# Differential attention on one Trainium2 core: score rows read in two-bank pieces, the one-piece maximum left by the read, lambda multiplied on GpSimd

## The reference, cut to what matters

```python
def _diff_attention(q, k, v, lq1, lk1, lq2, lk2, g_sub, lambda_init):   # 4 heads, 2 components of width 64, L = 2064
    lam = exp(sum(lq1 * lk1)) - exp(sum(lq2 * lk2)) + lambda_init
    def blk(qp, q1b, q2b):                       # 128 query rows at a time
        bias = where(mask, -slopes * dist, NEG)  # chunk-causal mask, ALiBi
        s1 = einsum('bhqd,bhkd->bhqk', q1b, k1) * scale + bias
        s2 = einsum('bhqd,bhkd->bhqk', q2b, k2) * scale + bias
        a = softmax(s1) - lam * softmax(s2)
        return einsum('bhqk,bhkv->bhqv', a, v)
```

## Time and profile before

| what | us |
|---|---|
| median of three runs (lowest, highest) | 2634.56 (2634.42, 2636.75) |
| profiled execution, its own time | 2637.24 |
| its span | 2635.5 |
| PE busy, share of the span | 2570.9, 98% |
| DVE busy | 1620.1, 61% |
| ACT busy | 1211.2, 46% |
| POOL busy | 334.1, 13% |
| differential attention | 460 to 828 |

### The profile page before, as it was taken

How to read it: one execution, slowest core, us unless ns; L and a number is a source line. 1 busy time by engine, 2 the same in 40 slices (tenths; PEclk the granted TensorE clock), 3 DMA queues, 4 the chain that set the end, 5 groups by cost and what they waited for, 6 DMA issues and landing times.

```text
span 2635.5 us, 35377 instructions
## 1 busy us (share of the span) xinstructions
PE 2570.9 (98%) x12220; PEld 2115.3 (80%) x12220; DVE 1620.1 (61%) x3488; ACT 1211.2 (46%) x2177; POOL 334.1 (13%) x366
## 2 busy tenths in 40 slices
PE   8999999899998999999999999999999999999998
PEld 8998787666676888877877888888888888888886
DVE  6223304989995766763458777777767565564665
ACT  6112312677775555554445333443335353343554
POOL 2110001222221222220000000000000001111133
PEclk9999999899999999999999999999999999999999
DMA  7324456633533011016576677666746355676787
GB/s 228 126 105 123 114 167 231 152 92 86 125 133 92 29 45 41 25 60 189 176 247 203 209 237 226 216 180 206 225 118 218 108 210 120 154 179 153 202 169 136
DMA packets 331516, 398.85 MB, mean 151 GB/s; under 512 B 23488, under 2 KB 237744, under 8 KB 323024
## 3 DMA queue, kind: packets, MB, share of 16 engines
q1 hardware_dynamic: 313776, 364.68, 44.1%
q0 software_dynamic: 17568, 31.99, 8.4%
HBM read 240.13 MB, written 156.48 MB: 150 GB/s over the span
## 4 chain that ended last, share of the span: by engine, by line
PE 62%; DVE 2%; DMA 1%; ACT 1%; issue 1%; SPq 0%; POOL 0%; DVEq 0%; ACTq 0%; POOLq 0%
PE ff_ps_x L3165 25%; PE ff_ps_m L3165 13%; PE ff_ps_z L3165 6%; PE ml_ps_s L2042 6%; PE ff_ps_m L1602 4%; PE ml_ps_o L2071 4%; PE ml_ps_t L2055 2%; DMA ml_v_raw<-scr_yT 1%; DMA ff_pieces<-scr_acc 0%; PE ff_ps_r L2602 0%; PE mo_ps_t L2619 0%; SPq L2229 0%; DVE ff_pieces L2332 0%; DVE ff_pieces L2523 0%; DVE ff_pieces L2519 0%
## 5 line engine op out<-in xcount | busy, mean ns | idle before, releaser
L3165 PE MATMUL ff_ps_x<-ff_mv_hi_p,ff_st_hi_p 128*128 128x512 f32 x764 | 297.9, 390 | 0.5 <-ACT ff_u L2905 0.5
L3165 PE MATMUL ff_ps_x<-ff_mv_hi_p,ff_st_lo_p 128*128 128x512 f32 x764 | 297.3, 389 | 0.0
L3165 PE MATMUL ff_ps_x<-ff_mv_lo_p,ff_st_hi_p 128*128 128x512 f32 x764 | 297.2, 389 | 0.0
L2042 PE MATMUL ml_ps_s<-wide,ml_qs 128*128 128x416 f32 (+14 forms) x880 | 197.9, 359 | 2.9 <-PEq L137 2.7
L3011 DVE TENSOR_TENSOR ff_st_lo_p<-ff_ps_m,ff_st_hi_p 128x512 fp32r<-128x512 f32 x190 | 130.6, 688 | 103.7 <-ACT ff_st_hi_p L2888 103.7
L2855 POOL DMA_DIRECT2D scr_acc<-ff_pieces x64 | 55.5, 872 | 1015.3 <-DVE ff_pieces L3035 946.8
L2905 ACT ACTIVATE ff_u<-ff_ps_x 128x512 f32<-128x512 f32 x128 | 76.6, 598 | 214.7 <-PE ff_ps_x L3165 214.7
L3165 PEld LDWEIGHTS ff_ps_x<-ff_mv_hi_p,ff_st_hi_p 128*128 128x128 f32 x764 | 143.4, 188 | 32.4 <-issue 2.0
L2042 PEld LDWEIGHTS ml_ps_s<-wide,ml_qs 128*128 128x128 f32 x880 | 152.5, 193 | 18.8 <-issue 7.4
L3165 PEld LDWEIGHTS ff_ps_x<-ff_mv_hi_p,ff_st_lo_p 128*128 128x128 f32 x764 | 143.4, 188 | 29.9
L3165 PEld LDWEIGHTS ff_ps_x<-ff_mv_lo_p,ff_st_hi_p 128*128 128x128 f32 x764 | 143.4, 188 | 29.6
(11 more groups left out here) (300 smaller groups left out, 6370.1 us busy)
## 6 DMA issues: line engine op xcount, KB each, us to landing
st_raw<-in_w_ff SPq DMA_DIRECT2D x64, 512.0 KB, 6.3
scr_hid<-ff_pieces SPq DMA_DIRECT2D x128, 256.0 KB, 2.6
st_raw<-scr_hid SPq DMA_DIRECT2D x64, 512.0 KB, 5.2
ring<-in_w_ff SPq DMA_DIRECT2D x28, 1024.0 KB, 7.8
scr_t<-ring SPq DMA_DIRECT2D x24, 1024.0 KB, 6.4
ring<-scr_t SPq DMA_DIRECT2D x21, 1024.0 KB, 7.9
scr_acc<-ff_pieces POOLq DMA_DIRECT2D x64, 256.0 KB, 4.0
ring<-scr_u SPq DMA_DIRECT2D x13, 1024.0 KB, 8.5
```

The lines of the kernel that those rows point to most:

```text
L2042: m = pe.matmul(ps_s[n % NSB][:, 0:w], q, k, start=j == 0, stop=j == len(pairs) - 1)
L3165: m = pe.matmul(bank[:, :], w[kind][:, k], a[kind][:, k], start=start and k == 0 and i == 0, stop=stop and k == KH - 1 and i == 2, skip_gr ...
```

## The change

Rows are cut by `row_pieces` into pieces of at most 1024 columns, two banks: 1 for rows 0 to 6, 2 for 7 to 14, 3 for row 15; 26 per component, 52 per head. `NSB` is 2, each of 1024 columns, so the scores still take four banks. `bank_parts` splits a piece wider than 512 into two parts on either side of the bank border, for which PE runs two matmuls each, with one semaphore for the piece; DVE reads both banks in one instruction. The read scales by -scale and takes the minimum, so that for one-piece rows its accumulator is `nmax` itself, and ACT waits for the read; rows of several pieces keep the combining instruction. The second sum is inverted in a step of its own (`ratio`, `RATIO_AFTER` 2), and POOL multiplies it by -lambda. `SCALE_AFTER` is 1 and `END_AFTER` 3, counted in pieces, and pending steps of earlier rows are put in only at the end of component 1. A piece costs w + 120 in the planner, before w + 60.

```diff
+def row_pieces(i):
+    width = META + P * (i + 1)
+    n = -(-width // 1024)
+    step = -(-width // n // 32) * 32
+    return [(c, min(step, width - c)) for c in range(0, width, step)]
+
+def bank_parts(w):
+    if w <= 512:
+        return 0, [(0, w)]
+    front = -(-w // 64) * 32
+    return 512 - front, [(0, front), (front, w - front)]
...
-        NSB = 4
-        ps_s = [mem.ps(f"da_ps_s{i}") for i in range(NSB)]
+        NSB = 2
+        ps_s = [mem.ps(f"da_ps_s{i}", 1024) for i in range(NSB)]
...
+        in_pieces = [(i, c) for i in range(NT) for c in range(COMPS) if len(row_pieces(i)) > 1]
...
-                        steps += [step for _, step in later if step[2] - NT * step[1] < i]
-                        later = [(left, step) for left, step in later if step[2] - NT * step[1] >= i]
+                        if c == COMPS - 1:
+                            steps += [step for _, step in later if step[2] - NT * step[1] < i]
+                            later = [(left, step) for left, step in later if step[2] - NT * step[1] >= i]
                         later.append((1, ("exp", 0, i, c)))
                         if c == 0:
                             later.append((SCALE_AFTER, ("scale", 0, i)))
                         if c == COMPS - 1:
+                            later.append((RATIO_AFTER, ("ratio", 0, i)))
                             later.append((END_AFTER, ("end", 0, i)))
...
-                return chunks[step[2]][3] + 60
+                return chunks[step[2]][3] + 120
...
-        SCALE_AFTER, END_AFTER = 2, 5
+        SCALE_AFTER, RATIO_AFTER, END_AFTER = 1, 2, 3
...
+            def ratio(h, i, **at):
+                if isinstance(h, int) and (h, i) == (0, 0):
+                    pool.wait_ge(lam_step, 4)
+                hold(pool, inv2_made, NT * h + i + 1)
+                pool.tensor_scalar(inv2[:, i % 2:i % 2 + 1], inv[:, i % 2, 1:2], lam[:, 3:4], 1.0, ALU.mult, ALU.mult).then_inc(ratio_ready, 1)
...
-                act.wait_ge(max_ready, NT * COMPS * h + COMPS * i + c + 1)
-                act.activation(comp_row(i, c, u), comp_row(i, c, u), ACT.Exp, bias=nmax[:, i % 2, c:c + 1], scale=scale,
+                if (i, c) in in_pieces:
+                    act.wait_ge(max_ready, len(in_pieces) * h + in_pieces.index((i, c)) + 1)
+                else:
+                    act.wait_ge(scores_read, NCH * h + [chunk[:2] for chunk in chunks].index((i, c)) + 1)
+                act.activation(comp_row(i, c, u), comp_row(i, c, u), ACT.Exp, bias=nmax[:, i % 2, c:c + 1], scale=-1.0,
...
+                if c == 1 and k0 == 0 and not (first_head and i < 2):
+                    dve.wait_ge(probs_ready, NT * h + i - 1)
+                least = mx[:, i % 2, c, nth:nth + 1] if (i, c) in in_pieces else nmax[:, i % 2, c:c + 1]
+                s0 = bank_parts(w)[0]
...
-                if k0 + w == META + P * (i + 1):
+                dve.tensor_tensor_reduce(out=comp_row(i, c, u)[:, k0:k0 + w], in0=ps_s[n % NSB][:, s0:s0 + w],
+                                         in1=bias[u][:, b0:b0 + w], scale=-scale, scalar=-LOWEST,
+                                         op0=ALU.add, op1=ALU.min, accum_out=least).then_inc(scores_read, 1)
+                if k0 + w == META + P * (i + 1) and (i, c) in in_pieces:
...
-                dve.tensor_scalar(inv2[:, i % 2:i % 2 + 1], inv[:, i % 2, 1:2], lam[:, 3:4], None, ALU.mult).then_inc(inv2_step, 1)
-                dve.wait_ge(inv2_step, n + 2)
+                dve.reciprocal(inv[:, i % 2, 1:2], total[:, i % 2, 1:2]).then_inc(inv2_made, 1)
+
+            def end(h, i, u, **at):
                 dve.wait_ge(first_scaled, NT * h + i + 1)
+                dve.wait_ge(ratio_ready, NT * h + i + 1)
...
-                for j in range(2):
-                    m = pe.matmul(ps_s[n % NSB][:, 0:w], qs[:, g % 2, c, P * b:P * b + P], keys[u][:, 2 * c + j, k0:k0 + w],
-                                  start=j == 0, stop=j == 1)
+                s0, parts = bank_parts(w)
+                for a, size in parts:
+                    for j in range(2):
+                        m = pe.matmul(ps_s[n % NSB][:, s0 + a:s0 + a + size], qs[:, g % 2, c, P * b:P * b + P],
+                                      keys[u][:, 2 * c + j, k0 + a:k0 + a + size], start=j == 0, stop=j == 1)
```

More of the change, by code:

```diff
@@ L1160, in attention @@
         inv_ready, first_scaled, probs_ready = (mem.sem(f"da_{s}") for s in ("inv_ready", "first_scaled", "probs_ready"))
-        inv2_step = mem.sem("da_inv2_step")
+        inv2_made, ratio_ready = mem.sem("da_inv2_made"), mem.sem("da_ratio_ready")
         pT_ready, pv_done = mem.sem(f"da_pT_ready"), mem.sem("da_pv_done")
@@ L1165, in attention @@
         o_stored = ahead.o_stored
-        chunks = [(i, c, k0, n) for i in range(NT) for c in range(COMPS) for k0, n in row_chunks(i)]
+        chunks = [(i, c, k0, n) for i in range(NT) for c in range(COMPS) for k0, n in row_pieces(i)]
         NCH = len(chunks)
+        in_pieces = [(i, c) for i in range(NT) for c in range(COMPS) if len(row_pieces(i)) > 1]
         tiles_of = lambda g: 1 + 4 * (g + 1)
@@ L1404, in scaled @@
                 pool.tensor_scalar(row(i, u), row(i, u), inv[:, i % 2, 0:1], 1.0, ALU.mult, ALU.mult).then_inc(first_scaled, 1)
-            heads(pool, {"scale": scaled})
+            def ratio(h, i, **at):
[3 more added lines that the diff above has]
+                pool.tensor_scalar(inv2[:, i % 2:i % 2 + 1], inv[:, i % 2, 1:2], lam[:, 3:4], 1.0, ALU.mult, ALU.mult).then_inc(ratio_ready, 1)
+            heads(pool, {"scale": scaled, "ratio": ratio})
         @stage.scalar
@@ L1454, in chunk @@
                 b0 = (NT - 1 - i) * P + k0
+                if c == 1 and k0 == 0 and not (first_head and i < 2):
+                    dve.wait_ge(probs_ready, NT * h + i - 1)
+                least = mx[:, i % 2, c, nth:nth + 1] if (i, c) in in_pieces else nmax[:, i % 2, c:c + 1]
+                s0 = bank_parts(w)[0]
                 hold(dve, scores_ready, NCH * h + n + 1)
[L1457 to L1460, removed]
-                if k0 + w == META + P * (i + 1):
+                dve.tensor_tensor_reduce(out=comp_row(i, c, u)[:, k0:k0 + w], in0=ps_s[n % NSB][:, s0:s0 + w],
+                                         in1=bias[u][:, b0:b0 + w], scale=-scale, scalar=-LOWEST,
+                                         op0=ALU.add, op1=ALU.min, accum_out=least).then_inc(scores_read, 1)
+                if k0 + w == META + P * (i + 1) and (i, c) in in_pieces:
                     dve.wait_ge(scores_read, NCH * h + n + 1)
-                    dve.tensor_scalar(nmax_all[:, 0:nth + 1], mx[:, i % 2, c, 0:nth + 1], -scale, None, ALU.mult, ALU.min,
+                    dve.tensor_scalar(nmax_all[:, 0:nth + 1], mx[:, i % 2, c, 0:nth + 1], 1.0, None, ALU.mult, ALU.min,
                                       accum_out=nmax[:, i % 2, c:c + 1]).then_inc(max_ready, 1)
@@ L1489, in invert, with invert_second @@
                 dve.reciprocal(inv[:, i % 2, 0:1], total[:, i % 2, 0:1]).then_inc(inv_ready, 1)
-            def end(h, i, u, **at):
+            def invert_second(h, i, **at):
                 if isinstance(h, int) and (h, i) == (0, 0):
                     minus_lambda()
-                n = 2 * (NT * h + i)
                 dve.wait_ge(exp_ready, NT * COMPS * h + COMPS * (i + 1))
-                dve.reciprocal(inv[:, i % 2, 1:2], total[:, i % 2, 1:2]).then_inc(inv2_step, 1)
-                dve.wait_ge(inv2_step, n + 1)
-                dve.tensor_scalar(inv2[:, i % 2:i % 2 + 1], inv[:, i % 2, 1:2], lam[:, 3:4], None, ALU.mult).then_inc(inv2_step, 1)
-                dve.wait_ge(inv2_step, n + 2)
+                dve.reciprocal(inv[:, i % 2, 1:2], total[:, i % 2, 1:2]).then_inc(inv2_made, 1)
+            def end(h, i, u, **at):
                 dve.wait_ge(first_scaled, NT * h + i + 1)
+                dve.wait_ge(ratio_ready, NT * h + i + 1)
                 dve.scalar_tensor_tensor(out=row(i, u), in0=comp_row(i, 1, u), scalar=inv2[:, i % 2:i % 2 + 1], in1=row(i, u),
                                          op0=ALU.mult, op1=ALU.add).then_inc(probs_ready, 1)
-            heads(dve, {"chunk": chunk, "scale": invert, "end": end})
+            heads(dve, {"chunk": chunk, "scale": invert, "ratio": invert_second, "end": end})
             dve.wait_ge(probs_ready, NT * H)
```

## The result

| | us |
|---|---|
| before, median of its runs (lowest, highest) | 2635.65 (2634.42, 2637.01) |
| changed kernel, median (lowest, highest) | 2659.28 (2655.82, 2662.52) |
| ratio, 95% interval | 1.009 [1.0076, 1.0103] |
| forecast | 2621.5 (2607 to 2638); chance given to "slower": 0.12 |

The change makes the kernel 0.9% slower, some 24 us. The forecast had the sign wrong and the time lies outside its range. In the trace of the changed kernel each head begins with its first read of row 0 at 462.22, 546.59, 640.77 and 734.62 us, and the next stage's first read is at 857.95; before these were 461.05, 540.35, 627.64, 714.95 and 832.06. So every head is longer: by 5.1, 6.9, 6.5 and 6.2 us. The profiled execution of the changed kernel took 2660.01 us. All executions behind the times here ran undisturbed but one of e8's ten, which took 13061.02 us and moves e8's median by 0.2 us.

The account below looks back on a forecast made before the run. Neither PE nor DVE alone was taken to bound the full heads; DVE paced the first. Three full heads gave 8 us and the first 5, 13 in all: from 2634.56 to 2621.6, put at 2621.5, range 2607 to 2638.

Parts of the forecast that it names:

- The step that failed: Rows 0 to 6 and 15: first sum's reciprocal waits for its exponential; 0.3 us for seven rows, 2.1 a head.
- four rivals: Slower by the ring, 0.14; POOL taking the place and hidden anyway, together 0.18; larger gain from steps and waits, 2609, 0.15.
- Three counts: 49 parts a component, 20 more matmuls a head; 12 reads fewer in the first phase; row 6 grouped with rows 0 to 5.
- DVE's terms: Work DVE sheds per head: reads 3.2 us, combining instructions 2.5, second sum's multiply 5.3; together 11, 44 in the stage.
- the trip: DVE to POOL and back for lambda's multiply, from the reciprocal's end to L1502: 0.16 + 0.19 + 0.11 = 0.46 us.
- The value of DVE's time: How much DVE relief shortens the stage: 44 us of DVE work were turned into 13 net, 0.3 for one.
- The sum of 13 us: Whole stage gain: 2.6 us a full head, 8 for three, plus 5 for the first head.
- The first head: DVE sets the pace beside rows 0 to 7, which have no turns; this head gains 5 us.
- the third rival: Hidden anyway: PE bounds the full heads, only the first head gains; 2632.5 us; chance 0.18 together with the second.
- The first rival: Two-slot ring stalls PE behind each `end`, 0.55 us at 40 ends; slower, 2647 us; chance 0.14.
- the ring as the cause: Sign: PE's waits on reads in a full head rising above 6.2 us would point to the two-slot ring.
- The second rival: POOL's `scale` starts before L1502 in seven rows a head, costing DVE 20 us; 2631 us; chance 0.18 together with the third.

Follow-up runs that it names:

- e8: Changed kernel with SCALE_AFTER 2 in place of 1 and lambda multiplied on DVE in the `ratio` step; 2636.74 us, ratio 1.0.
- e2: Changed kernel with the exponential put into the list at once at the end of its row and component, not one piece later; 2635.59 us, ratio 0.9999.
- e1: Changed kernel with SCALE_AFTER 2 in place of 1, so the first sum's reciprocal stands one piece later; 2635.63 us, ratio 1.0002.
- e9: Kernel before, with L1502 subtracting on only the first half of each row's columns, the rest left out; 2624.62 us, ratio 0.9958.
- e6: Changed kernel with one-bank chunks, four slots, planner cost w + 60 and SCALE_AFTER, RATIO_AFTER, END_AFTER 2, 3, 5; 2630.7 us, ratio 0.9981.
- e3: Kernel before with NSB 2 in place of 4, same one-bank chunks and order; 2694.4 us, ratio 1.0222.
- e13: Changed kernel with pending steps of earlier rows put in at the end of either component again; 2658.4 us, ratio 1.009.
- e4: Kernel before with one-chunk maximum left by the read, lambda on POOL in a `ratio` step, and the new `probs_ready` wait; 2644.6 us, ratio 1.0033.

## Why the prediction was wrong

**The step that failed** is in the part on what DVE is given: "That reciprocal waits for an exponential which starts when the read before last ended [...] about 0.3 us short", seven rows a head, 2.1 us, with a bound of 5.3, and nothing for rows 7 to 14. In the second head DVE waited 6.1 us for rows 0 to 6 and 7.6 for the others, 13.7 in all; in the stage 45.8 where I had 8.4. A full head took 94.2 us, where I had named 82 to 83. The error is not in a duration but in "starts when the read ended". The exponential starts when ACT reaches it, and ACT's list has copies ahead of it (two in row 4, three in row 11), each bound to a turn that PE makes after the next scores. I had the full step list and read DVE's column of it only, and none of my four rivals named this wait. e2 moves just the exponential and gives 24 us back; e1 moves just the first component's `scale` step, the reciprocal with POOL's multiply behind it, and gives 24 us back.

Three counts in the prediction are wrong, too little to matter. The parts of a component are 48, not 49 (64 more matmuls in the program, not 80). The first phase of a head has 10 reads fewer, not 12. And row 6 belongs with rows 7 to 14: its `ratio` and `end` have a read between them (574.28 and 575.18).

**DVE's terms** were nearly right. 144 fewer reads: the CUSTOM_DVE_ANT_0 and its accumulator fall from 218.6 us to 196.0 for the stage's busy time, and a read of 672 columns over the bank border takes 0.78 to the next start (587.76 to 588.54), 0.70 of columns and 0.08 fixed. The combining instructions are 72, as said. In busy time, though, a full head sheds 7.6 us (79.0 less 71.3), where the terms say 11 and I had named 67 for what is left. A part of the terms was never busy time: of the 0.33 us for L1498, 0.21 is. POOL's multiply was under-priced: 0.268 in place of 0.192, so the trip is about 0.54 (0.16 + 0.27 + 0.11) and not 0.46.

**The value of DVE's time** held in size: 0.28 by e9. The sum of 13 us was thus about what the change might have given without any new wait. e1 shows that with the worst wait gone it gives 0. What takes the 13 us is in part argued: e1 has waits for the trip to POOL (15.3 us, but e8, without them, is no faster), for the second sum (11.3, before 7.3), and the pieces cost 1 to 5 us. The first head did get faster in e1 and e6, as the forecast said of the change: 77.3 and 76.3 us against 79.3. The full heads did not: 87.4 and 88.5 in e1, against 87.3. For the mended kernel that looks like the third rival, "hidden anyway"; for the changed kernel, whose first head took 84.4, it says nothing.

**The first rival** came nearest in time (2647), for another reason. Its sign was there: PE's waits on reads in a full head rose from 6.2 to 11.5 us (10.3 and 1.2), and I had written that this would show the ring as the cause. It does not: in e1, with the same ring, they are back at 34.2 in the stage (24.0 + 10.2; before 36.7). A wait for a slot says that DVE was late, not why. e3 shows that a ring can cost 59 us. In this change, with the order mended, ring and pieces together cost 1 to 5 us net of what 144 fewer reads give back; no run has the ring's part alone.

**The second rival** was real but small. Where POOL's multiply and L1538 stand side by side, the one that starts second is held up. The first view is the timeline of the first head, where POOL starts 0.04 us sooner; the second is POOL's line in the stage for 144 columns:

```profile
472.26 0.82 POOL L1426 TENSOR_SCALAR da_rows<-da_rows,da_inv 128x656 f32<-128x656 f32 x1
...
472.30 1.33 DVE L1538 SCALAR_TENSOR_TENSOR da_rows<-da_second,da_inv,da_rows 128x528 f32<-128x528 f32 x1 [0.20 <-POOL da_inv L1433]
```

```profile
L1426 POOL TENSOR_SCALAR da_rows<-da_rows,da_inv 128x144 f32<-128x144 f32 x4 | 7.9, 1981 | 5.7 <-DVE da_inv L1525 5.3
```

L1538 of 528 columns takes 1.33 us there, and 0.77 where it starts first. It ends 0.55 us after POOL does, which is its 528 columns at 1.044 ns, as if it had begun only then. The mean of 1.98 us in the second view mixes two cases: POOL's 144 columns took 0.39 us in the first head and 2.51 in each of the other three, where they started 0.03 us behind L1538 of 2064 columns. By the rule of the Trainium skill ("SBUF — State Buffer", on SBUF's two separate sides) this is an exclusive lock; the trace agrees in kind. As argued against it, L1538 is mostly first, and over the stage DVE loses 2 us by it (L1538 89.5 us against 87.6). POOL loses 13.4 (89.5 against 76.1).

**The clock** was not in the prediction, and may hold a part of the loss. In the second phase it is 0.91 where it was 1.00. It is lowered at 507 to 511, 599 to 607, 640 to 644, 695 to 699 and 787 to 795 us; before, it was not lowered anywhere from 489 to 830. PE had stood 1.78 us, until 598.47, before the second of these stretches, and was busy without a gap while it lasted. One less the granted clock, added up in steps of 1 us from 462 to 870 us, gives 18.7 us in the changed kernel and 11.9 before. So, as an estimate from one trace each, the clock can account for up to 7 of the 24 us. It is not needed for a loss of this size: e13, 23 us slower, has 11.9 as before.

## What to carry to other kernels

- Before an instruction is moved earlier in a list that several in-order engines walk, follow what it waits for through the queue of the engine that makes it, and through what that engine's queue waits for in turn. The distance that counts is not from the input's end but from the point where the maker gets to it.
- When units of a plan are made larger, distances that are counted in units change by unlike amounts: here a constant halved from 2 to 1 for pieces up to twice as long looked right in columns for the read, and was wrong for the copies that the planner lays between.
- A kernel that leaves some work out (e9) prices a relief before the change is built: 0.28 us for 1. It prices the relief only; it says nothing of the waits that the change adds, and those decided here.

## What the runs showed that I had not expected

- Lambda's multiply on one column takes POOL 0.268 us, against 0.192 for the 128x1 multiply of the earlier trace rows; the trip DVE to POOL and back is about 0.54, more than the 0.45 from the reciprocal's start to L1502 that DVE took with its own multiply; counted in the same way, e4's row 8 takes 0.69.
- Halving the score ring of the kernel before cost 59 us, when its four slots had shown only 11.9 us of idle PE for reads.
- After PE had stood 1.78 us, the granted clock was 0.50 from 600 to 606 us, with PE busy all the while; no run separates what brought it down.
